# Projections, constant table, lambda transfers and gate products: five moves in a two-block transformer kernel

## What is computed

```python
c_act = silu(c)
mod = c_act @ w_ada + b_ada                  # six modulation vectors
y = concatenate([a, r]) @ w_out              # project "wo"
x = layer_norm(ALPHA * x + gt1 * y, ...)
...
lam = exp(sum(lq1 * lk1)) - exp(sum(lq2 * lk2)) + lam_init
h = h + concatenate([da_out, gla_out]) @ w_o     # project "wo2"
h = h + o @ w_co                                 # project "co2"
...
gate = p_g * top_p / sum(top_p)              # two experts per token
out = (silu(xb @ w_gate[e]) * (xb @ w_up[e])) @ w_down[e]
y[token] += out * gate
```

## Time and profile before

| | |
|---|---|
| median of 3 runs | 3235.31 us (3234.71 to 3235.44) |
| profiled execution, its time | 3234.4 us |
| profiled execution, its span | 3232.6 us |
| mean granted clock of TensorE | 0.968 |
| PE busy | 2967.9 us, 92% of the span |
| DVE busy | 1853.9 us, 57% |
| ACT busy | 1147.1 us, 35% |
| POOL busy | 479.0 us, 15% |
| DMA moved | 363.49 MB |

### The profile page before, as it was taken

One profiled execution on the slowest core, in us unless ns is written; L12 is line 12 of the kernel. 1 busy time (PEld: TensorE's weight loads), 2 busy tenths in 40 slices (PEclk: granted clock), 3 DMA queues, 4 the chain that ended last, 5 costly groups with the idle time before them and its releaser, 6 DMA issues.

```text
span 3232.6 us, 36440 instructions
## 1 busy us (share of the span) xinstructions
PE 2967.9 (92%) x14880; PEld 2252.3 (70%) x14880; DVE 1853.9 (57%) x2766; ACT 1147.1 (35%) x1784; POOL 479.0 (15%) x307
## 2 busy tenths in 40 slices
PE   7999699988999999979998997799998969999998
PEld 3445476887888888865455985595556958887777
DVE  5775756566443444464356436621123369999998
ACT  2111344323122111112233334512233247777776
POOL 1012400005111000031000000000000016433333
PEclk9999899999999999989999999899999979999999
DMA  8320100011111111103000110203002279999996
GB/s 309 105 79 20 43 1 1 27 54 52 53 51 41 44 48 53 52 26 131 0 1 16 38 40 1 79 1 130 27 1 61 93 284 367 388 384 379 382 376 262
DMA packets 129535, 363.49 MB, mean 112 GB/s; under 512 B 14394, under 2 KB 66776, under 8 KB 104784
## 3 DMA queue, kind: packets, MB, share of 16 engines
q1 hardware_dynamic: 112832, 330.19, 28.0%
q0 software_dynamic: 16528, 30.89, 2.7%
HBM read 356.82 MB, written 29.38 MB: 119 GB/s over the span
## 4 chain that ended last, share of the span: by engine, by line
PE 65%; DVE 12%; DMA 11%; ACT 6%; issue 4%; POOL 2%; SPq 0%; POOLq 0%; DVEq 0%; ACTq 0%
PE PS L180 60%; DMA MR<-in_w_e_up 3%; DMA MR<-in_w_e_down 3%; PE PS L191 3%; DMA MR<-in_w_e_gate 3%; DVE ML L2799 1%; PE PS L571 1%; ACT BIG L2166 1%; ACT MH L2794 1%; DVE BIG L819 1%; DVE ST L2193 1%; DVE BIG L2220 1%; DMA BIG<-in_w_ada 0%; POOL XR L1559 0%; DVE XR L1531 0%
## 5 line engine op out<-in xcount | busy, mean ns | idle before, releaser
L180 PE MATMUL PS<-BIG 128*128 128x512 f32 (+9 forms) x2704 | 782.6, 456 | 38.4 <-ACT BIG L2166 11.4
L180 PEld LDWEIGHTS PS<-BIG 128*128 128x128 f32 (+4 forms) x2704 | 398.6, 189 | 346.3 <-issue 295.5
L2799 DVE TENSOR_TENSOR ML<-MR,MH 128x2048 fp32r<-128x2048 f32 x144 | 329.8, 2303 | 28.8 <-ACT MH L2794 28.1
L180 PE MATMUL PS<-MH,MX 128*128 128x512 f32 x1024 | 322.8, 397 | 12.2 <-DVE ML L2799 10.2
L2794 ACT CAST MH<-MR 128x2048 fp32r<-128x2048 f32 x144 | 275.4, 1914 | 93.2 <-DMA MR<-in_w_e_up 44.1
L191 PE MATMUL PS<-CT,BIG 128*128 128x128 f32 (+4 forms) x1080 | 164.3, 290 | 81.6 <-DVE BIG L2220 24.5
L180 PEld LDWEIGHTS PS<-MH,MX 128*128 128x128 f32 x1024 | 190.2, 190 | 56.9 <-DVE ML L2799 17.3
L191 PEld LDWEIGHTS PS<-CT,BIG 128*128 128x128 f32 (+4 forms) x1080 | 124.3, 144 | 148.6 <-ACT BIG L1112 34.1
L180 PE MATMUL PS<-FWH,FHH 128*128 128x512 f32 x512 | 203.5, 397 | 17.5 <-DVE FWL L1401 10.8
L180 PE MATMUL PS<-FXH,FWH 128*128 128x512 f32 x512 | 200.9, 392 | 7.1 <-DVE FWL L1401 7.1
L180 PE MATMUL PS<-FWL,FHH 128*128 128x512 f32 x512 | 202.3, 395 | 0.0
(11 more groups left out here) (456 smaller groups left out, 5870.0 us busy)
## 6 DMA issues: line engine op xcount, KB each, us to landing
MR<-in_w_e_gate SPq DMA_DIRECT2D x50, 1024.0 KB, 19.1
MR<-in_w_e_up SPq DMA_DIRECT2D x48, 1024.0 KB, 21.1
MR<-in_w_e_down SPq DMA_DIRECT2D x46, 1024.0 KB, 19.5
FWR<-in_w_ff SPq DMA_DIRECT2D x32, 1024.0 KB
XR<-in_w_e_down SPq DMA_DIRECT2D x18, 1024.0 KB, 18.7
BC<-in_w_ada SPq DMA_DIRECT2D x32, 512.0 KB, 3.6
XR<-in_w_e_up SPq DMA_DIRECT2D x16, 1024.0 KB, 20.9
XR<-in_w_e_gate SPq DMA_DIRECT2D x14, 1024.0 KB, 19.3
```

The lines of the kernel that those rows point to most:

```text
L180: ins = pe.matmul(o, l, r, start=(start and n == 0), stop=(n == len(pairs) - 1), skip_group_check=True)
L2799: dve.tensor_tensor(cut_at(ML, i), raw(i), cut_at(MH, i).bitcast(F32), ALU.subtract).then_inc(e.w_lo.up(), 1)
```

## The change

1. The three projections: PE does 12 turns, then product 0, turns 12 and 13, product 1, turns 14 and 15, and on. ACT and DVE cut weight quarter 0 after turn 7, quarter 1 after turn 15.
2. The order of products: after the first 16 come (2,0), (2,1), (3,0), (3,1), and then (2,t), (3,t) from t = 2. `row_done` counts accordingly (19 for row 0, otherwise 18 + 2t).
3. The constant table is reordered (identity, ones and `inv` first) and comes in two transfers: 304 columns where the whole was, and 1691 columns behind the latent weights, ahead of the retention weights. POOL, PE, ACT and DVE wait for the second at the retention.
4. The lambda vectors go to one partition; one small matmul with a row of ones (`pe_lambda`, in the latent product after t = 4) and a DVE copy (after t = 5) spread the result.
5. `dve_gates` moves ahead of the first rows of the experts; PE's sums of the gates move from step 0 to step 1.

```diff
-            sp.dma_start(CT[:, :], cst).then_inc(cst_in.up(), 16)
+            sp.dma_start(CT[:, 0:CST1], cst[:, 0:CST1]).then_inc(cst_in.up(), 16)
...
-                gps.dma_start(lam4[:, n, :], X[s][0].partition_broadcast(128)).then_inc(lam_in.up(), 16)
+                gps.dma_start(lam4[:, n, :], X[s][0].rearrange("(a n) -> a n", a=1)).then_inc(lam_in.up(), 16)
...
+        def pe_lambda():
+            P.wait_ge(*nl_ok[1])
+            P.wait_ge(*cols_ok[1])
+            mm(PS[:, 7, 0:1], [(C("one")[0:1, :], nl1)]).then_inc(nl_mm.up(), 1)
...
         def sp_ret():
+            sp.dma_start(CT[:, CST1:], cst[:, CST1:]).then_inc(cst2_in.up(), 16)
             S.wait_ge(*mod_mm[3])
...
-            steps = [(n, t) for n in range(2) for t in range(8)] + [(n, t) for t in range(8) for n in (2, 3)]
+            steps = [(n, t) for n in range(2) for t in range(8)] + [(2, 0), (2, 1), (3, 0), (3, 1)] + [
+                (n, t) for t in range(2, 8) for n in (2, 3)]
...
             def pe_project():
-                for m in range(16):
...
+                for m in range(12):
+                    pe_turn(m)
...
+                    if k_ < 2:
+                        pe_turn(12 + 2 * k_)
+                        pe_turn(13 + 2 * k_)
...
+                    if m == 7:
+                        act_cut(0)
-                for i in range(4):
+                for i in range(1, 4):
                     act_cut(i)
...
+                    if m == 7:
+                        dve_cut(0)
                 V.wait_ge(*x_tr[16])
-                dve_cut(0)
                 dve_cut(1)
...
-                if e is main and j == 0:
+                if e is main and j == 1:
                     pe_gate_slots()
...
-                if e is main and j == 0:
-                    dve_gates()
...
             dve_wcut(main, 0)
             dve_wcut(main, 1)
+            dve_gates()
             dve_rows(main, 0)
```

More of the change, by code:

```diff
@@ L41, in const_table @@
         "ident": np.eye(128),
+        "one": np.ones((128, 128)),
+        "inv": np.tile(np.concatenate([10000.0 ** (-np.arange(32) / 32), 10000.0 ** (-np.arange(16) / 16)])[None], (128, 1)),
         "caus": np.where(i <= j, 0.0, NEG),
@@ L50, in const_table @@
         "mf": (same & (j > i)).astype(float),
-        "inv": np.tile(np.concatenate([10000.0 ** (-np.arange(32) / 32), 10000.0 ** (-np.arange(16) / 16)])[None], (128, 1)),
         "su": (j < i).astype(float),
-        "one": np.ones((128, 128)),
         "io": np.tile(np.arange(128.0)[None], (128, 1)),
@@ L231, in program @@
         lam_ok, cs_ok, ang_ok, sin_ok = by_dve("lam_ok"), by_dve("cs_ok"), by_dve("ang_ok"), by_act("sin_ok")
-        c_in = landed("c_in")
+        c_in, cst2_in = landed("c_in"), landed("cst2_in")
+        CST1 = sum(CONSTS[n_][1] for n_ in ("ident", "one", "inv"))
+        nl_ok, nl_mm, nlam_ok = by_dve("nl_ok"), by_pe("nl_mm"), by_dve("nlam_ok")
         w_ada, b_ada = X["w_ada"][0], X["b_ada"][0]
@@ L575, in pe_lat @@
                     pe_ada_unit(u)
+                if t == 4:
+                    pe_lambda()
         def act_lat():
@@ L698, in program @@
         bank[0], bank[1], bank[2], bank[3] = lat_cp[5], lat_cp[6], lat_cp[7], lat_cp[8]
-        bank[5] = ar_ok[2]
+        bank[5], bank[7] = ar_ok[2], nlam_ok[1]
         close(ln_var, ln_std, ab1_ok, lat_sq, lat_ms, lat_std)
@@ L1167, in program, with row_done @@
         close(rs_std, rs_var, lt_pe, lt_ev, ro_n, rs_ok, latn_ok, kr_ok, r_sta, r_silu, r_add)
-        close(*x_t, cst_in, cols_in, pos_in, lam_in, c_in, *ada_in, *aq_in, *ab_in, *ar_out, aq_w, aq_mm, ar_ok)
+        close(*x_t, cst_in, cst2_in, nl_ok, nl_mm, cols_in, pos_in, lam_in, c_in, *ada_in, *aq_in, *ab_in, *ar_out, aq_w, aq_mm, ar_ok)
+        def row_done(t):
+            return 18 + 2 * t if t else 19
         def project(tag, x_mm, wd, src, scale_of, areas, first_load, pe_ready, act_ready, dve_ready, dve_evac, evac_done,
@@ L1193, in sp_project, with pe_turn @@
                                      w_in_[i % 2].up(), 16)
-            def pe_project():
-                for m in range(16):
[L1197 to L1202, removed]
+            def pe_turn(m):
+                th, c = divmod(m, 8)
+                pe_ready(th, c)
+                P.wait_ge(*(x_ok[m - 3] if m >= 4 else bank[m]))
+                for u in range(4):
+                    ins = tr(PS[:, m % 4, 128 * u:128 * u + 128], src(4 * th + u, c))
+                ins.then_inc(x_tr.up(), 1)
+            def pe_project():
+                for m in range(12):
+                    pe_turn(m)
                 for k_, (n, t) in enumerate(steps):
@@ L1356, in sp_ff @@
             for i in range(32):
-                S.wait_ge(*(fc_lo[i - 1] if i >= 2 else wo_mm[18]))
+                S.wait_ge(*(fc_lo[i - 1] if i >= 2 else wo_mm[row_done(0)]))
                 sp.dma_start(chunk(FWR, i), chunks[i].rearrange("(k p) n -> p k n", p=128)).then_inc(fw_in[i % 2].up(), 16)
```

23 lines of the change are left out of this document (16 added, 7 removed).

## The result

The changed kernel takes 3201.97 us (median of 4 runs, 3201.66 to 3202.98), beside 3235.01 us for the kernel before on the same chip (3232.52 to 3235.44): a ratio of 0.990 with an interval of 0.9883 to 0.9917, 33.0 us less. The forecast was 3211.0 and its range ended at 3204: the sign was right, the gain was a third larger than the forecast's.

The account below looks back on a forecast made before the run. TensorE, busy 92%, was taken to bound most of the kernel, transfers the very start and the experts; 2.3 + 11.1 + 4.5 + 6.5 = 24.4 us off 3234.4 gave 3210.0, median 3210.9, rounded to 3211; range 3204 to 3219.

Parts of the forecast that it names:

- Start: -2.3: Lambda transfers and table: quarter 0 of w_ada lands 2.4 us sooner and TensorE's run follows; net 2.3 us off.
- I take 2.4, the smaller, since it is a delay of one transfer and not a mean over all: Lambda's cost at the start: 2.4 us from x's tile arrivals, chosen over 2.7 us from transfer rates.
- the bound of 4.5: Start's upper bound: 4.5 us gained, where DVE's sum binds again, if quarter 0's last share is hit most.
- the cover by DVE: DVE's sum of quarter 3 gains 4.5 us (2.4 lambda, 2.1 table), so it stays covered and doesn't hold TensorE back.
- Split turns: -11.1: Weight quarter 0 cut amid the turns in three projections: 3.7 us each, 11.1 us off, pause left about 2.5 us.
- The credit for the clock: Shorter pause ahead of product 0 saves a third of the mean 1.75 us slow-clock loss: 0.6 us per projection.
- the clock stays high through all three projections: Rival: the halved pause brings no slow clock, another 1.15 us three times: 3207.5; chance 0.12.
- Order: -4.5: New product order removes TensorE's idle 1.50 us before (3,0): 1.5 us in each of three projections, 4.5 us off.
- the forecast's nothing: Feed-forward part, started by the projection's own end: gains pass through, with 0 us of gain of its own.
- Gates: -6.5: Expert step 0: expert 1 starts 6.9 us sooner, the ring moves on; 6.5 us off, the middle of 5.5 to 7.5.
- the bound of 7.5: Gates' upper bound: first raw buffer free 7.5 us sooner, with the slow clock after the pause gone.
- the transfers absorb it: Rival: the transfer-bound expert stage gives nothing back, keeping 1 us of 6.5: 3216.5; chance 0.12.

Follow-up runs that it names:

- lambda_alone: Kernel before with only the lambda edit: four vectors to one partition, a matmul and a DVE copy spread the result; 3230.56 us against 3235.75, ratio 0.9983.
- split_alone: Kernel before with only the first weight quarter cut amid the turns and the last four turns between products, in all three projections; 3221.03 us, ratio 0.9943.
- after_again: The changed kernel once more, unaltered, traced a second time; 3199.80 us against 3235.20 for the kernel before.
- order_alone: Kernel before with only the new order of products and its row_done numbers, in all three projections; 3229.61 us, ratio 0.9977.
- dose2: Changed kernel plus two unused spreads of 256 bytes to 128 partitions ahead of POOL's other small vectors; 3205.65 us.
- early0: Changed kernel with weight quarter 0 cut still earlier: in wo ahead of the first scaling, in co2 ahead of the waits for the attention; 3201.86 us.
- late4b: Changed kernel plus four unused spreads behind POOL's small vectors, which DVE waits for only after quarter 3's sum; 3210.80 us.

## Why the prediction was right or wrong

- **Start: -2.3 forecast, -7.2 in the trace, 4.5 us alone by medians, and 6 to 9 when lambda alone is undone.** The step that failed is "I take 2.4, the smaller, since it is a delay of one transfer and not a mean over all". The reading was right for its place: tile 1 of x lands at 8.55 us before and at 6.38 after, 2.2 us late. What failed is carrying it over to quarter 0. The spreads' packets ran on until 13.6 us, and while the median part of quarter 0 was late by 2.0 us, the last one was late by 5.2, and TensorE waits for the last. The text had named this case, "if the last of its 16 shares is the one that is hit most", but kept it as the bound of 4.5. The same 2.4 sits in the cover by DVE: quarter 3 was to land 2.4 + 2.1 = 4.5 us sooner. It lands 4.4 us sooner by lambda alone, 2.3 by the table alone and 7.0 with both. So the bound was too low as well, and that lambda_alone gains 4.5 at the latent product agrees with it by coincidence. Of the 7.2 us, 5.2 are this transfer, priced at 2.4; 1.3 are the luck of the first 16 matmuls, and 0.7 come later.
- **Split turns: -11.1.** Each step is in the trace: the pause 2.26, product 0 9.16 us after the first scaling, the bank's wait 0.25, 11.8 us by the landmarks of split_alone. The credit for the clock, 0.6 us each, 1.8 in all, came out near: with 2.88 us as the measure for each product, the 16 products of each of the three chain rows before lose 6.5 us together, and product 0 after the change 5.0, a credit of 1.4. The forecast's own 2.3, 1.7 and 1.3 us sum to 5.3, since its measure was 0.121 us for a matmul and not the 0.120 of this row (2.88 us for 24). The forecast set this credit against the Trainium skill, "TensorE: Matmul & The Clock Gate", part 1, by which the throttled state is the default and activity releases it, and drew from it that every pause that counts is paid afresh. In the trace of the result this holds three times out of three, and in after_again once. Over all traces product 0 is slow behind each of the 18 pauses of 4.96 us and behind 18 of the 27 of 2.26 to 2.7 us. So the trace is still divided on pauses of this length, as the forecast said. Its rival (the clock stays high through all three projections) came in no trace; two of three is the most.
- **Order: -4.5.** The three pauses are gone, 4.5 us; 4.0 or 5.6 by the landmarks, 6.1 by the medians; none has come behind (3,0). The second pause of the feed-forward part grows from 6.95 to 7.97 us. That looks like this edit's, since order_alone has it (8.09) and split_alone doesn't (6.82). It goes with the clock: the traces in which TensorE stays slow longer behind the pause before it, of 7.10 us, have 7.8 to 8.1 us, the others 6.7 to 7.0, and dose2 alone, at 8.9, is an exception. But the clock does this in nine of the eleven traces with the new order (not in dose2 and early0) and in none of the six without. In these nine the products behind that pause make up for it, 2.0 us sooner, so the forecast's nothing was off by 1 us of gain.
- **The projections together: -15.6.** 15.1 in the trace of the result, 19.2 in after_again, 17.7 in the mean over the traces: 2 us too small in the mean.
- **Gates: -6.5.** 7.3 in the trace, 7.4 alone by medians (an interval of 4.2 to 10.0), 6.5 in the mean over the traces. Expert 1 starts 6.7 us sooner after the routed rows (6.9 forecast). The ring of weight buffers moves on with the first buffer that comes free and gives the pause back; the runs can't choose between the middle and the bound of 7.5. That the transfers absorb it is out.
- **The Trainium skill, "DMA: Bandwidth & Descriptors", rules for kernel authors**, asks for large transfers; by the forecast's estimate from the skill's table the split of the constants would have been a loss of under 1 us. No run shows that loss; the split lands quarter 3 sooner, by 2.3 us, and beside lambda gains 0.8 to 1.7 us at the latent product.
- **The range.** Its lower end held the high clock, the start's 4.5 and the experts' 7.5, and came to 3204.2. What it lacked is the start: 7.2 us against the bound of 4.5, which would have put it at 3201.5. Two sums of the prediction are slightly off, without effect on this: 24 matmuls at half the clock are 5.8 us and end product 0 at 612.7, not 612.0, and the lower bound of 4 us for a projection takes 3.6 us off three of them, not 3.

## What to carry to other kernels

A transfer that is waited for ends with its last part: to price what disturbs it, look at when its parts land, first, median and last, and not at a mean rate or at an earlier transfer. A number that every partition needs was better computed on one partition here and spread by a matmul than worked out from vectors fetched 128 times, and putting the fetches later moved the harm to another transfer. A single trace can't place a gain of under 3 us in a stage; the same kernel traced twice gave 15.1 and 19.2 us for the same three stages. Work that an engine could do in its idle time gains nothing while it stands behind a waiting instruction of that engine's list: place it ahead of the wait, and check that it doesn't delay what frees the banks.

## What the runs showed of the hardware

A spread of 256 bytes to 128 partitions is 16 packets of 2048 bytes, and they take 577 (before) to 1178 ns (dose2) in the mean and up to 2.3 us (late4b), 6 to 13 times the 89 ns of an ordinary packet of that size; with four spreads under way the engines were busy to 0.85 and moved 157 GB/s (late4b). They spread the landings of one transfer's 16 parts over 5 us instead of 1.3 (before and after). The other surprise is how differently TensorE's clock follows the same pause: the same instructions behind the same pause of 3.06 us ran at full clock in some traces and lost 1.4 or 2.9 us in others, and both happened to the changed kernel itself. That is enough to hide or to double a gain of 3 us in a single trace. The runs of the kernel before lie between 3229.69 and 3239.68 us (24 runs on one chip), and the clock goes with them: the two at a mean granted clock of 0.969 take 3231.9 us in the mean, the two at 0.965 take 3238.2.
